# Scoring 32 more tokens of an expert layer by gathered rows: dense scores on 352 columns instead of 384, with low halves split on Pool and three smaller rewrites

## The reference

```
qry = (h @ w_query).reshape(B, S, PEER_HEADS, 2, PEER_HALF)
sc = jnp.einsum('bshpd,hpnd->bshpn', qry, sub_keys)
top_s, top_i = lax.top_k(sc, K)
...
best, flat = lax.top_k(cand.reshape(B, S, PEER_HEADS, K * K), K)
...
g = jax.nn.softmax(best.astype(jnp.float32), axis=-1).astype(h.dtype)
...
u = expert_u[et]
act = jax.nn.gelu(jnp.einsum('td,tkd->tk', xt, u), approximate=False) * gt
return jnp.einsum('tk,tkd->td', act, expert_v[et])
```

## Time and profile before

| | us |
|---|---|
| median of three runs | 1722.82 |
| profiled execution, whole | 1722.1 |
| its span, first to last instruction | 1720.3 |
| PE busy | 1686.5 |
| DVE busy | 1359.0 |
| ACT busy | 717.7 |
| POOL busy | 638.1 |

### The profile page before, as it was taken

The page is one execution under the profiler, slowest core; times in us unless marked ns, Lnnn a source line. Parts: engine busy times, 40 slices in busy tenths (PEclk is TensorE's granted clock), DMA queues, the critical chain, the costliest instruction groups (busy, mean ns, idle before and its releaser), DMA issues.

```text
span 1720.3 us, 24226 instructions
## 1 busy us (share of the span) xinstructions
PE 1686.5 (98%) x8795; PEld 1490.6 (87%) x8795; DVE 1359.0 (79%) x2770; ACT 717.7 (42%) x1119; POOL 638.1 (37%) x372
## 2 busy tenths in 40 slices
PE   6999999999999999999999999999999999999998
PEld 4688777878899999999999999999999988888886
DVE  7347546674589998999999498888878799989897
ACT  3356455443443433444444333333333343333334
POOL 0322222235356674611111055555434463334331
PEclk9999999999999999999999999999999999999999
DMA  8222332433143433567777899999998899999993
GB/s 342 98 98 86 128 154 86 147 122 136 42 138 113 148 127 101 196 213 286 283 266 266 299 403 349 326 372 332 333 325 299 273 391 413 390 382 391 381 374 110
DMA packets 137068, 417.97 MB, mean 243 GB/s; under 512 B 13072, under 2 KB 58128, under 8 KB 131088
## 3 DMA queue, kind: packets, MB, share of 16 engines
q1 hardware_dynamic: 88592, 266.87, 42.3%
q0 software_dynamic: 36864, 134.23, 21.2%
q10 hardware_dynamic: 11520, 15.73, 2.5%
HBM read 373.80 MB, written 42.99 MB: 242 GB/s over the span
## 4 chain that ended last, share of the span: by engine, by line
PE 82%; DVE 15%; issue 2%; ACT 1%; DMA 1%; POOL 0%; SPq 0%; ACTq 0%
PE bank L944 30%; PE bank L897 22%; PE bank L684 10%; PE bank L843 5%; PE bank L932 5%; PE bank L630 1%; PE bank L710 1%; DVE arena L1595 1%; DVE idx L1534 1%; DVE arena L1556 1%; DVE arena L1548 1%; PE bank L773 1%; DVE arena L1549 1%; DVE slots L1527 1%; PE bank L752 1%
## 5 line engine op out<-in xcount | busy, mean ns | idle before, releaser
L897 PE MATMUL bank<-h_split,u_split 128*128 128x384 f32 x3072 | 556.9, 337 | 2.2 <-DVE u_split L1511 1.9
L897 PEld LDWEIGHTS bank<-h_split,u_split 128*128 128x128 f32 x3072 | 534.7, 188 | 8.5 <-DVE u_split L1511 2.3
L944 PE MATMUL bank<-v_late,a_late 128*128 128x512 f32 x1440 | 326.7, 389 | 0.0
L944 PEld LDWEIGHTS bank<-v_late,a_late 128*128 128x128 f32 x1440 | 270.3, 188 | 55.9
L589 POOL DMA_INDIRECT rows<-eu,idx x128 | 176.6, 1380 | 366.1 <-DVE dots L1516 343.8
L589 POOL DMA_INDIRECT rows<-ev,idx x128 | 173.7, 1357 | 244.1 <-DVE row_sum L1622 211.6
L562 POOL TENSOR_TENSOR block_split<-arena,block_split 128x1024 fp32r<-128x1024 f32 x48 | 117.1, 2443 | 310.1 <-ACT block_split L1010 310.1
L1159 ACT ACTIVATE gelus<-bank 128x384 f32<-128x384 f32 x128 | 62.9, 491 | 371.4 <-PE bank L897 371.3
L944 PE MATMUL bank<-v_split,a_split 128*128 128x512 f32 x864 | 205.4, 391 | 0.0
L944 PEld LDWEIGHTS bank<-v_split,a_split 128*128 128x128 f32 x864 | 161.6, 188 | 31.8
L1622 DVE SCALAR_TENSOR_TENSOR row_sum<-rows,agate,row_sum 128x1024 f32<-128x1024 f32 x127 | 162.6, 1280 | 4.4 <-DVE row_sum L1622 0.5
(11 more groups left out here) (251 smaller groups left out, 2395.2 us busy)
## 6 DMA issues: line engine op xcount, KB each, us to landing
u_raw<-euT SPq DMA_DIRECT2D x128, 512.0 KB, 7.1
v_raw<-ev SPq DMA_DIRECT2D x128, 512.0 KB, 6.8
arena<-w_blocks SPq DMA_DIRECT2D x50, 512.0 KB, 8.8
arena<-w_ada SPq DMA_DIRECT2D x12, 2048.0 KB, 8.1
gates_scratch<-stage SPq DMA_DIRECT2D x24, 1024.0 KB, 10.9
gates<-gates_scratch SPq DMA_DIRECT2D x32, 768.0 KB, 9.2
gelu_scratch<-gelus ACTq DMA_DIRECT2D x80, 192.0 KB, 3.6
gelus<-gelu_scratch SPq DMA_DIRECT2D x80, 192.0 KB, 8.5
```

What stands on the lines that cost most here:

```text
L897: last = pe.matmul(ps[6 + b][:, 0:TD], us[:, b, wp, k * P:(k + 1) * P], hs[:, xp, k, 0:TD], start=(k == 0 and q == 0), stop=(k == DC - 1 a ...
L944: last = pe.matmul(ps[2 * t + f][:], a[:, ap, t * P:(t + 1) * P], v[:, vp, f * 512:(f + 1) * 512], start=(first and q == 0), stop=True, sk ...
```

## The change

In words, with the stretch that each part touches:

- Tokens 352 to 383 (`E` = 32) leave the dense scores: `scores` streams `TE` = 352 columns. Their 32 x 128 scores come from 32 more gathers (`NE`) and dot products with a copy of these tokens' rows, `hE`, repeated four times over the partitions, so that one gather serves four experts of each of the 32 tokens. GELU and gate are multiplied into the gate rows ahead of the one-hot matrices, and the columns of `gel` that belong to them are 1.0, so `values` stays as it was.
- In the one-hot stage Pool makes the low parts instead of VectorE, and does its gathers in between. The dots stand otherwise: 32 new ones and 4 of the old in the one-hot stage, 12 in the 7 chunks before the value loop, 112 in the value loop, in 36 steps; 38 accumulations in its last 11 steps.
- The constant 0..127 (`iota`) is copied into PSUM for `hot`, and `hot_j` becomes a tensor_scalar with two scalar columns. In `rank` several small operands move to PSUM (`first_values`, `den`, `row_b`, `whole`), and the row index is computed once at the end instead of in each rank.
- The products for the adaptive norm are folded on VectorE (a transposition and a sum, `ada_fold`) and summed by four matmuls in all, in the `up` stage. The squares of the `out` blocks are added on VectorE and summed over partitions once.

The core of the diff:

```
+E = 32
+TE = TD - E
+NE = P * E // P
...
-DOTS_BY = 34
-ACC_FROM = 35
-ACC_F = 34
+MORE_DOTS = 4
+LAST_DOTS = 12
+DOTS_G = MORE_DOTS + LAST_DOTS
+DOTS_BY = 36
+ACC_FROM = 37
+ACC_F = 38
+E_DOTS, E_GELU, E_GATES, E_TURN = 26, 27, 28, 30
...
+def dots_beside(s):
+
+    if s <= E_DOTS:
+        return NE * s // E_DOTS
+    return NE + MORE_DOTS * (s - E_DOTS) // (BESIDE - E_DOTS)
...
-            for g in range(DOTS_RANK, 2 * P):
+            for g in range(NG):
+                gather(g)
+            pool.wait_ge(u_split, EARLY + 2)
+            for k in range(BESIDE):
+                u_low(EARLY + 2 + k)
+                for g in range(NG + dots_beside(max(0, k - 1)), NG + dots_beside(k)):
+                    gather(g)
+            for g in range(NG + dots_beside(BESIDE - 1), NE + 2 * P):
                 gather(g)
...
-                if n:
-                    ada_sum(n + 2, n % 2, ps[2], 252 + 4 * n)
...
-                if kind == "out" and m:
-                    rms_sum(DC, squares2, [m - 1])
-            rms_sum(DC, squares2, [DC - 1])
+                if kind == "up" and m == 3:
+                    later_products()
+            pe.wait_ge(squares_added, DC - 2)
...
-                        last = pe.matmul(ps[6 + b][:, 0:TD], us[:, b, wp, k * P:(k + 1) * P], hs[:, xp, k, 0:TD],
+                        last = pe.matmul(ps[6 + b][:, 0:TE], us[:, b, wp, k * P:(k + 1) * P], hs[:, xp, k, 0:TE],
...
-                    if c == TT:
+                    if c == 0:
                         pe.wait_ge(h_split, DC + 1)
-                        turn(c, h, TT - 1)
+                        turn(TT, h, TT - 1)
+                    if c == 1:
+                        pe.wait_ge(turned, 2 * TT + 3)
+                        for f in range(2):
+                            for j in range(4):
+                                last = pe.transpose(ps[4 + f][:, j * P:(j + 1) * P], hX[:, 4 * f + j, :], ident)
+                            last.then_inc(turn_done, 1)
...
+            act_(iota, cst[:, K_IOTA:K_IOTA + P], ACT.Copy).then_inc(slotsT_ready, 1)
...
+            def ada_fold(n):
+
+                step(nv.transpose(adap[:, 1, :], adap[:, 0, :]))
+                nv.tensor_reduce(ada_parts[:, n, :], adap[:, 1, :].rearrange("p (c r) -> p c r", c=16), AX.X, ALU.add).then_inc(ada_ready, 1)
...
-                    row_index(i - 1)
-
+
+                if i == 0:
+                    ve.wait_ge(turned, 2 * (TT + 1) + 3)
+                step(nv.tensor_copy(first_values, tv[:, 0, :, :]))
...
-                    ins = nv.scalar_tensor_tensor(ohj[:, b, q, :], cst[:, K_IOTA:K_IOTA + P], slotsT[:, 1, t:t + 1],
-                                                  slotsT[:, 2, t:t + 1].to_broadcast([P, P]), ALU.is_equal, ALU.mult)
+                    ins = nv.tensor_scalar(ohj[:, b, q, :], iota, slotsT[:, 1, t:t + 1], slotsT[:, 2, t:t + 1],
+                                           ALU.is_equal, ALU.mult)
...
             for c in range(EARLY, EARLY + BESIDE):
-                u_low(c + 2)
-                if (c - EARLY) % 3:
-                    dot(DOTS_RANK + 2 * ((c - EARLY) // 3) + (c - EARLY) % 3 - 1)
+                s = c - EARLY
...
+                for k in range(dots_beside(s), dots_beside(s + 1)):
+                    dot(k)
...
             for c in range(EARLY + BESIDE, STASHED):
                 u_low(c + 2)
+                s = c - EARLY - BESIDE
+                for k in range(LAST_DOTS * s // BEFORE, LAST_DOTS * (s + 1) // BEFORE):
+                    dot(NE + MORE_DOTS + k)
```

More of the change, by code:

```diff
@@ L316, in build @@
         shifted = carve(2, TT * TOPK).bitcast(U32)
-        shiftedf = carve(3, TT * TOPK)
+        row_a = carve(TT * TOPK)
+        row_b, whole = (ps[4][:, TT * TOPK * f:TT * TOPK * (f + 1)] for f in range(2))
+        first_values = ps[5][:, 0:TT * TOPK].rearrange("p (t k) -> p t k", t=TT)
+        den = ps[5][:, TT * TOPK:TT * TOPK + 2 * TT]
         edge = carve(2, TT * TOPK)
@@ L642, in ada_sum @@
                 for m in range(4):
-                    last = pe.matmul(bank[:, bass.ds(col + m, 1)], adap[:, b, m * P:(m + 1) * P], ones[:, 0:1], start=(n < 3 and m == 0), stop=True, skip_group_check=True)
+                    last = pe.matmul(bank[:, bass.ds(col + m, 1)], adap[:, b, m * P:(m + 1) * P], ones[:, 0:1], start=(m == 0), stop=True, skip_group_check=True)
                 last.then_inc(ada_summed, 1)
@@ L815, in _, with later_products @@
                     turn_values(i + 1)
-            ada_sum(HEADS + 2, 0, ps[2], 256 + 4 * (HEADS - 1))
+            def later_products():
+                pe.wait_ge(ada_ready, 3 + 2 * HEADS)
+                of_32 = ada_parts.rearrange("p n (m b) -> p n m b", m=4)
+                for b in range(4):
+                    last = pe.matmul(ps[4][:, 0:32].rearrange("p (n m) -> p n m", n=HEADS), cst[:, K_FOLD + 96 - 32 * b:K_FOLD + 224 - 32 * b],
+                                     of_32[:, :, :, b], start=(b == 0), stop=(b == 3))
+                last.then_inc(ada_summed, 1)
             pe.wait_ge(oa_out, HEADS)
             pe.wait_ge(ob_out, HEADS)
-            pe.wait_ge(mod_ready, 2)
             pe.wait_ge(gate_kept, 2 * DC)
@@ L845, in _ @@
                 last.then_inc(block_done, 1)
-                if kind == "out" and m:
-                    rms_sum(DC, squares2, [m - 1])
-            rms_sum(DC, squares2, [DC - 1])
+                if kind == "up" and m == 3:
+                    later_products()
+            pe.wait_ge(squares_added, DC - 2)
+            for t in range(TT):
+                pe.matmul(ps[7][:, t:t + 1], square_sum[:, t * P:(t + 1) * P], ones[:, 0:1], start=(t == 0), stop=False, skip_group_check=True)
+            pe.wait_ge(sq_ready, 2 * DC)
+            for t in range(TT):
+                last = pe.matmul(ps[7][:, t:t + 1], square[:, t * P:(t + 1) * P], ones[:, 0:1], start=False, stop=True, skip_group_check=True)
+            last.then_inc(sq_summed, 1)
+            pe.wait_ge(mod_ready, 2)
             def turn(j, a, t):
@@ L1600, in _ @@
                 rank(i, finish_before=i > 0)
-            for k in range(DOTS_HEAD * (HEADS - 2), DOTS_RANK):
-                dot(k)
             ve.wait_ge(u_split, POOL_U)
@@ L1773, in constants @@
     k[:, K_EPS] = EPS
+    s = np.arange(32)
+    for a in range(4):
+        k[32 * a + s, K_FOLD + 96 + s] = 1.0
     return k
```

182 lines of the change are left out of this document (117 added, 65 removed).

## The result

The changed kernel takes 1700.76 us (median of four runs, 1700.26 to 1702.75), the kernel before 1722.95 beside it: a ratio of 0.9877, interval 0.9865 to 0.9889. It is 22 us faster where 39.0 were forecast, inside the stated range of 1669 to 1703. The profiled execution took 1700.5 us, 1698.6 of them span.

The account below looks back on a forecast made before the run. TensorE, busy 98% of the span, was taken to bound the kernel. Gains of 53.0 us less costs of 14.0 gave 39.0 off 1722.1, so 1683 us, range 1669 to 1703.

Parts of the forecast that it names:

- rival B: Value loop: DMA sustains at most 353 GB/s, so a step stays at 8.35 us; time 1702 us, chance 0.10.
- the narrower scores: Dense scores: 32 columns less save 13.4 ns a matmul over 3072 matmuls, -41.2 us (bounds 0 and 41.2).
- the adaptive norm: Attention heads: seven sums of 0.81 us leave TensorE's line, -5.7 us; the eighth already lies in a gap.
- the one-hot stage: One-hot stage: TensorE needs 6.22 us a chunk against 6.56 before, VectorE 5.61, so no waits added.
- the stall before the loop: Seven chunks before the value loop: twelve gathers on a nearly full DMA stall TensorE, +9.0 us (0 to 18.7).
- Rival C: Dense scores: weight loads pace 352 columns, so narrowing gains nothing; time 1722 us, no change, chance 0.04.
- The squares: `out` blocks: the sums of squares of six blocks leave TensorE's line, less 0.8 for `later_products`, -4.6 us.
- The ranks: Ranking stage: shorter VectorE ranks give nothing inside the stage and -1.5 us at its end (0 to -3.8).
- the small operations: Start of the one-hot stage: six small operations stand ahead of the first `hot`, +1.6 us (0 to 3).
- Rival A: One-hot stage: every dot waits 2.42 us for Pool's subtraction, making VectorE the bound; time 1748 us, chance 0.11.
- The chunks before the loop: Seven chunks before the value loop: 7.3 us of gather stall plus 1.7 at half clock, +9.0 us.
- The value loop: Value loop: a TensorE step falls from 8.28 to 7.96 us; accumulations in the last 11 steps add +2 (0 to 6).

Follow-up runs that it names:

- the first experiment: The kernel before with only the scores narrowed to 352 columns, the 32 tokens' scores left out: 1687.82 us, ratio 0.9795.
- The second experiment: The changed kernel with `hot_j` reading the constant 0..127 from SBUF instead of PSUM: 1739.24 us, ratio 1.0102 to the kernel before.

## Why the prediction was right, and by how much its terms were off

The time lies in the stated range in part by luck. The prediction's own sum gave 1699 at worst, and 1700.76 is above that; the range reached to 1703 because it took in rival B, which did not happen. The bound, the gain of the narrower scores and the kinds of cost were right. Of 39.0 us 17 are missing, 15 of them by three terms: the adaptive norm (4.2) and the one-hot stage (4.5), for which no bounds were given, and the stall before the loop (6.2), inside its bounds.

**The narrower scores: right.** The 2972 distances between neighbouring scores have a median of 160 ns (174 before), as two widths and a line gave. The columns alone brought 34 us, because PE then waited for other engines in the ranking and one-hot stages; in the changed kernel the value loop got its full share (-13.0, forecast -12.7). Rival C falls.

**The adaptive norm: mis-sized.** The step "seven stand in PE's line, so -5.7" was wrong for three of them. In the three heads with a rope PE waited for DVE already, and a sum taken from PE only lengthened that wait (0.72 to 1.60 us). That is 2.6 us; a further 1.1 us lie in the first 40 us, where 12 matmuls took 7.78 instead of 6.67 us, and 6.83 in another kernel with the same code there: chance. 5.7 - 2.6 - 1.1 is 2.0, measured 1.5; half a us stays open. The eighth sum lay in a gap, as the prediction says: without it PE's wait ahead of the first `up` matmul grew from 1.34 to 2.33 us, by the length of that sum, and brought nothing. Whether `ada_sum` stood in a wait was to be read from the row of the matmuls behind each one.

**The squares: right.** -4.0 for -4.6.

**The ranks: near in sum (-9.1 for -10.7), by another way.** PE still waits 1.7 us at the end for `u_low(36)`, but the 24 matmuls behind it take 4.13 us instead of 6.00. "PE does not wait for ranks inside the stage, so this gives nothing there" was read from the old scores: the first experiment shows that with narrower scores and the old ranks Pool's low parts hold PE up for 3.6 us inside the stage. That the sum came near is luck. Before the first one-hot matrices PE then waits 0.94 us for the next low part, behind the small operations that the prediction priced at 1.6.

**The one-hot stage: the step that failed.** "Whether `iota` in PSUM changes 0.61 no row shows; ... it stays near" held for `hot_i` (0.60), and was silently carried over to `hot_j`, which went from 1.05 to 1.27 us a group. The second experiment shows that the source in PSUM does it. The prediction had named this as a sign that it would be wrong: operations that read PSUM take clearly longer than the same ones on SBUF. An average over 36 chunks hid the rest: 32 dots stand in the first 26. So DVE needs 6.51 us a chunk there, not 5.61, and PE's gain of 11.2 us becomes 6.7. Over 28 chunks the same dots gave 1.6 us back. Rival A's end state, DVE as the bound, came about without its mechanism: the 32 new dots never waited. None of them began inside one of Pool's subtractions, while three subtractions began inside a dot and took 2.47 to 2.78 us. In the kernel with `hot_i` from SBUF ten dots began inside one and waited, so the dots are not safe; why they fall well here no run shows.

**The chunks before the loop: right in kind, too small.** "About half of the gathers come ahead of the first blocks" was the assumption: 7.3 us and 1.7 of half clock. It cost as much as if all of them came ahead: 15.1 us against the kernel without them, of which 12.9 are PE's idle, inside the bounds of 0 to 18.7. DMA was full, and every load took longer: the last gates, issued at 942.63, landed 19.0 us later, and the first read of gates took 20.7, where the kernel without these gathers shows 12.6 and 8.6.

**The value loop: right.** 7.98 us a step for 7.96; rival B falls at 112 dots. With more dots something like it comes: at 124 dots PE waits 3.0 to 9.8 us in the loop and at 128 15.5, with a DMA share of 0.98 to 1.01 and 366 to 384 GB/s.

**Slips in the working.** The bounds that it prints for the terms behind the scores add up to 1701 at worst, not 1699; the time came near that by two terms that had no bounds. No line gives the 7.3 us of the stall; half of the gathers by its own numbers would be 15.6/2 + 2.9 - 1.6 = 9.1. The two ends that it calls equal to the tenth are 664.82 and 664.74. None of these changes the account above.

## What to carry to other kernels

Taking work off the bound engine pays only where that engine does not already wait: read the row behind each removed instruction for its idle time. A cost "near the same" needs a row for each operation that changes its operand, and the load on an engine is counted over the chunks where it stands, not over the stage. A range that holds only because it takes in a rival has not confirmed the sum. Before an instruction is moved, follow what its end releases: here a product on VectorE held a load on SP, and the loads behind it cost 25 us that moving two lines gave back.

## What was not expected of the hardware

A `tensor_scalar` of 128 x 128 elements took 0.32 us from PSUM and 0.26 from SBUF (four in 1.27 and 1.02), while a `tensor_tensor` of 128 x 512 with one operand in PSUM took 0.60, against 0.61 before with both in SBUF. And a `tensor_scalar` with a single tensor operand in SBUF was held up by Pool's subtraction just like operations with two, 2.49 us for four instead of 1.02; from PSUM it was not.
